# A decoder layer on one core: how the first expert's tokens are picked, where the softmax weights are made, and which row tile comes fourth

## The chip, the core and the metric

The kernel runs on one core of a Trainium2 chip. A core has TensorE (the matrix engine; the profile writes PE for its matmuls and PEld for its weight loads), VectorE (DVE), ScalarE (ACT), GpSimd (POOL), and a queue engine SP that only issues DMAs here. The engines run their own instruction streams and meet at semaphores. The metric is device time in microseconds; lower is better.

## What is computed

One layer of a decoder with 512 prompt rows and 64 sample rows of 1024 numbers, all in float32. Mixing (attention and spatial gating) comes first. The part that matters here starts with its output projection and ends in the expert layer:

```python
    mix = jnp.concatenate([a.reshape(B, S, ATT_W), s_out], axis=-1) @ w_out
    x = x + ga1 * rms_norm(mix, g_post_mix)
    h2 = rms_norm(x, g_pre_ffn) * (1 + sc2) + sh2
    f = hier_moe(h2.reshape(B * S, D_MODEL), ...)
...
def hier_moe(x, w_rg, b_rg, w_re, b_re, w_gate, w_up, w_down):
    g_logits = (x @ w_rg).astype(F32) + b_rg.astype(F32)
    g_prob = jax.nn.softmax(g_logits, axis=-1)
    g_idx = jnp.argmax(g_logits, axis=-1)
    g_w = jnp.take_along_axis(g_prob, g_idx[:, None], axis=-1)
    e_logits = ((x @ w_re).astype(F32) + b_re.astype(F32)).reshape(N, N_EXPERT_GROUPS, EXPERTS_PER_GROUP)
    e_in = jnp.take_along_axis(e_logits, g_idx[:, None, None], axis=1)[:, 0]
    top_p, top_i = lax.top_k(jax.nn.softmax(e_in, axis=-1), TOP_K_IN_GROUP)
    wts = top_p / jnp.sum(top_p, axis=-1, keepdims=True) * g_w
...
    for e in range(N_EXPERTS):
        hdn = jax.nn.silu(x @ w_gate[e]) * (x @ w_up[e])
        y = y + gates[:, e:e + 1] * (hdn @ w_down[e])
```

Each row picks one of four groups, then two of the four experts in it; there are 16 experts, each with 6 MB of weights (`w_gate` and `w_up` 1024 x 512, `w_down` 512 x 1024).

## The kernel before, in words

The program is written out by hand, engine by engine: each engine's function issues its instructions in the order in which they run, and each wait is a semaphore count. No planner sets an order. The stages are `condition`, `project`, `attend_prompt`, `attend_sample`, then `merge` and `experts` in one block, then `later_tiles` and `combine`. The change touches `merge` and `experts`.

**Merge, projection.** The 576 rows are five row tiles: 0 to 3 are the prompt's, 128 rows each, and 4 is the samples', 64 rows. For each tile TensorE transposes the mixed rows (`mix_tr`, L1573), ScalarE and VectorE copy half each out of PSUM (`evac_mix`), and TensorE multiplies with `w_out` (L1611, 32 records of 512 columns). For the samples' tile the two halves of the contraction run side by side on 64 columns each of the array (L1617), and VectorE adds them afterwards (L1425, L1426). Then ScalarE squares and sums (L1359), GpSimd makes the root (`power`, L737, L738), VectorE scales and adds the residual (L1435, L1436), ScalarE squares again (L1365), GpSimd again, and VectorE makes `h2` (L1441, L1442). `h2` is stored to DRAM, transposed on TensorE (`h2_tr_of`, L1584), copied out (L1331, L1397), and multiplied with the router's 20 columns (`logits_of`, L1594). A loop over t interleaves the tiles: TensorE issues projection t, transposes of `h2` t-1, transposes of the mix t+1, logits t-1. `h2` has two buffers `hv`, so ScalarE waits, before it writes one again, for the transposes and the store of the tile two before.

**Merge, routing.** From the logits of all tiles (one instruction covers them all, 128 partitions by 5 tiles by a few columns) VectorE picks the group and the two experts. `first_max` is four operations. In between it waits for ScalarE's two exponentials (L1371, L1373), makes the softmax weights (L1482 to L1486), and writes `hot`, the table of chosen experts (L1489 to L1491). TensorE turns `hot` into ranks, the number of earlier rows that chose the same expert (L1633, L1635). From ranks and totals VectorE orders the experts by their load, gives each a tile of slots, and writes for each row the tile `C` and the place in it `R` (L1496 to L1544). TensorE multiplies the two into a table: which token stands at each place of each tile (L1641). Cast to integers (L1547) it is what GpSimd gathers rows of `h2` with (L1718, L1721).

**Experts.** Sixteen tiles of slots (the first two for experts 0 and 1 at fixed places, then by load, of 128 and 64 rows in turn) run through a loop with two buffers each: gather, transposes (`tokens`, L1795), evacuation of half each (ScalarE L1738, VectorE L1764), gate product (L1812), up product (L1820), `silu` and product, transposes (L1856), down product (L1833) of the tile before, store. Weights go through six slots of the ring; SP issues a load as soon as the product that used the slot is done. The order after the first two experts comes from VectorE (L1553). `step` is in TensorE's order gate, up, next tile's transposes, down of the tile before, transposes of its own. `ORDER`, `first_tokens` and `table` don't exist yet.

## Time and profile before

| | us |
|---|---|
| three runs, median | 1033.86 |
| lowest, highest | 1033.08, 1035.77 |
| the profiled execution | 1031.1 |
| its span | 1029.3 |

| engine | busy, us | share of the span |
|---|---|---|
| TensorE matmuls | 825.5 | 80% |
| TensorE weight loads | 429.3 | 42% |
| VectorE | 345.0 | 34% |
| ScalarE | 210.0 | 20% |
| GpSimd | 121.7 | 12% |

The merge's projection starts at 562 us of the span, the routing at 655, the first expert's gate product at 688.8, and the last down product ends near 988.6. The rest is the combination. A matmul in f32 shows as two records, each with a weight load of its own; a transpose shows as one. In the timeline rows below the columns are start, duration, engine, line, operation, output<-input with the partitions and elements, and the count of merged records; the bracket gives the idle time before it and what ended it. TensorE's clock has two levels, 1.2 and 2.4 GHz; the windows give the granted share, where 0.50 is the lower one.

### The profile page before, as it was taken

The numbers are of one execution on the slowest core, as the hardware profiler recorded it, in microseconds if no ns is written. First come the engines' busy times: TensorE is split into PE (matmuls) and PEld (weight loads), VectorE is DVE, ScalarE is ACT, GpSimd is POOL, SyncE is SP. The second block draws the span as 40 slices with busy tenths as digits, with TensorE's granted clock in tenths as the row PEclk, the third lists the DMA queues.
The fourth block names the chain that finished last, engine by engine and source line by source line (L and its number), as shares of the span: only waits on it lengthen the run. The fifth ranks groups of instructions, "written<-read, shape, count | busy, mean of one in ns | idle before, by whom it ended". The sixth has DMA issues, their size and how long they took to land. (4 is left out here: it accounts for less than half of the span.)

```text
span 1029.3 us, 12324 instructions
## 1 busy us (share of the span) xinstructions
PE 825.5 (80%) x4656; PEld 429.3 (42%) x4656; DVE 345.0 (34%) x799; ACT 210.0 (20%) x437; POOL 121.7 (12%) x204
## 2 busy tenths in 40 slices
PE   0329999999788869899875999249998999999940
PEld 0024444444455545665642455234443444444410
DVE  0143630021578755555530354530110111001017
ACT  0200100100556423433420121100110111111113
POOL 1310100000400011322210010010000000000024
PEclk9959999999679889999986999559999999999975
DMA  8959412382892017999972951514789899999835
GB/s 258 253 165 348 169 56 77 118 305 65 316 401 65 1 61 309 389 414 425 378 285 113 337 223 61 205 62 173 273 327 411 354 388 399 377 415 379 346 115 192
DMA packets 49293, 257.52 MB, mean 250 GB/s; under 512 B 5704, under 2 KB 6952, under 8 KB 38880
## 3 DMA queue, kind: packets, MB, share of 16 engines
q1 hardware_dynamic: 30224, 151.54, 38.7%
q0 software_dynamic: 10672, 86.72, 22.1%
q10 hardware_dynamic: 8352, 18.66, 5.7%
q8 instruction: 29, 0.48, 0.2%
q14 instruction: 16, 0.13, 0.0%
HBM read 234.07 MB, written 22.83 MB: 250 GB/s over the span
## 5 line engine op out<-in xcount | busy, mean ns | idle before, releaser
L695 PE MATMUL ps<-sb 128*128 128x512 f32 x320 | 142.8, 601 | 0.0
L1820 PE MATMUL ps<-sb 128*128 128x512 f32 (+1 forms) x256 | 114.2, 599 | 0.0
L695 PEld LDWEIGHTS ps<-sb 128*128 128x128 f32 x320 | 60.3, 192 | 73.7 <-issue 73.3
L1122 PE MATMUL ps<-sb 128*128 128x128 f32 x512 | 64.9, 281 | 18.4 <-ACT sb L991 9.3
L1774 DVE TENSOR_TENSOR sb<-sb,ps 128x512 f32<-128x512 f32 (+1 forms) x16 | 10.9, 684 | 190.9 <-PE ps L1820 127.6
L1122 PEld LDWEIGHTS ps<-sb 128*128 128x128 f32 x512 | 56.7, 143 | 31.7 <-issue 17.4
L1812 PE MATMUL ps<-sb 128*128 128x512 f32 x144 | 66.8, 618 | 1.0 <-ACT sb L1738 0.8
L1833 PE MATMUL ps<-sb 128*128 128x512 f32 x144 | 63.5, 594 | 0.0
L1611 PE MATMUL ps<-sb 128*128 128x512 f32 x128 | 58.8, 619 | 1.9 <-DVE sb L1389 0.9
L1817 PE MATMUL ps<-sb 128*64 128x512 f32 x112 | 50.9, 608 | 7.5 <-DMA sb<-in_w_up 7.5
L1820 PEld LDWEIGHTS ps<-sb 128*128 128x128 f32 (+1 forms) x256 | 42.5, 168 | 34.4 <-issue 34.4
L879 PE MATMUL ps<-sb 128*128 128x128 f32 (+3 forms) x128 | 53.2, 556 | 3.2 <-ACT sb L792 3.2
L442 PE MATMUL ps<-sb 128*9 128x512 f32 x192 | 22.6, 624 | 39.6 <-DMA sb<-in_w_ada 39.6
L1038 DVE COPY sb<-ps 128x512 f32<-128x512 f32 x64 | 41.2, 685 | 21.0 <-PE ps L1122 21.0
L805 ACT ACTIVATE sb<-sb 128x128 f32<-128x128 f32 (+3 forms) x64 | 35.4, 554 | 41.9 <-DVE sb L859 41.9
L1812 PEld LDWEIGHTS ps<-sb 128*128 128x128 f32 x144 | 27.7, 198 | 33.7 <-issue 31.8
L991 ACT ACTIVATE sb<-ps 128x512 f32<-128x512 f32 x64 | 34.8, 595 | 32.3 <-PE ps L1122 32.0
L1833 PEld LDWEIGHTS ps<-sb 128*128 128x128 f32 x144 | 26.7, 190 | 31.0 <-issue 30.9
L1611 PEld LDWEIGHTS ps<-sb 128*128 128x128 f32 x128 | 25.1, 199 | 32.9 <-issue 30.4
L1781 DVE COPY sb<-ps 128x512 f32<-128x512 f32 (+1 forms) x16 | 11.1, 692 | 77.6 <-PE ps L1833 54.5
L1172 PE MATMUL ps<-sb 128*32 128x256 f32 x512 | 32.2, 404 | 5.8 <-DMA sb<-in_cache_v,ints 4.7
L1135 PE MATMUL ps<-sb 128*32 128x512 f32 (+1 forms) x320 | 36.6, 530 | 0.0
(254 smaller groups left out, 984.2 us busy)
## 6 DMA issues: line engine op xcount, KB each, us to landing
sb<-in_w_gate SPq DMA_DIRECT2D x16, 2048.0 KB, 12.5
sb<-in_w_up SPq DMA_DIRECT2D x16, 2048.0 KB, 16.9
sb<-in_w_down SPq DMA_DIRECT2D x16, 2048.0 KB, 8.4
sb<-in_w_ada SPq DMA_DIRECT2D x12, 2048.0 KB, 12.8
sb<-in_w_in SPq DMA_DIRECT2D x5, 2048.0 KB, 16.6
y_rows<-sb POOLq DMA_DIRECT2D x1, 5120.0 KB, 36.8
y_rows<-sb SPq DMA_DIRECT2D x9, 512.0 KB, 8.8
sb<-in_x_prompt ACTq DMA_DIRECT2D x8, 512.0 KB, 11.9
```

The lines of the kernel that those rows point to most:

```text
L695: last = pe.matmul(PS[:, n % 4, :], L.hT[:, k, t * P:t * P + P], w[:, k, :], start=k == 0, stop=k == KC - 1)
L805: act.activation(pb[n % 3][j][:, 0:w], pb[n % 3][j][:, 0:w], ACT.Exp, bias=nm[:, q:q + 1], accum_out=sums[:, q:q + 1]).then_inc(exp_done, 1)
L879: pe.matmul(PS[:, 2 * (n % 2) + j, 0:P * (i + 1)], qz[i % 2][:, h // 2, 2 * (h % 2) + j, :], L.kT[:, h // 2, 0:P * (i + 1)], start=True, s ...
L991: act.activation(kt[ch % 2][:, h, :], PS[:, h, :], ACT.Copy).then_inc(kt_act, 1)
L1038: dve.tensor_copy(kt[ch % 2][:, h, :], PS[:, h, :]).then_inc(kt_dve, 1)
L1122: last = pe.transpose(PS[:, h, P * g:P * g + P], kp[:, 4 * (ch % 2) + g, P * h:P * h + P], L.cst("ident"))
L1135: last = pe.matmul(bank[32 * h:32 * h + 32, 0:512 if ch < 4 else NS], qst[par][:, h, :], rhs, start=True, stop=True)
L1611: last = pe.matmul(PS[:, proj_bank(t, c), :], mixT[t % 2][:, k, :], w[:, k, :], start=k == 0, stop=k == KC - 1)
L1812: last = pe.matmul(PS[:, 0, :], x[:, k, :], w_gate[:, k, :], start=k == 0, stop=k == KC - 1)
L1817: last = pe.matmul(PS[n:P, 0, :], x[:, k, :], w_gate[:, k, :], start=k == 0, stop=k == KC - 1)
L1820: last = pe.matmul(PS[0:n, 1, :], x[:, k, :], w_up[:, k, :], start=k == 0, stop=k == KC - 1)
L1833: last = pe.matmul(PS[:, 5 + c, :], hT[:, k, :], w[:, k, 512 * c:512 * c + 512], start=k == 0, stop=k == FC - 1)
```

## The change

It does four things. The samples' tile comes fourth and row tile 3 last (`ORDER`); the loops count positions i, and t is the tile at that position. `h2` gets five buffers, on the mixed rows, which are not needed once transposed; the scratch of the routing and the late loads `ga` move elsewhere for it. The softmax weights are made behind the selection instead of inside it, while TensorE makes the ranks. And the tokens of expert 0, whose place is fixed, are no longer gathered with the table: VectorE makes from their ranks a matrix with a one where row and place meet (`first_row`), and TensorE multiplies `h2` with it (`first_tokens`, 40 matmuls), which gives the tokens transposed. The table product moves behind the first gate product, and the gathers start with tile 1. The diff, cut to its core:

```diff
 COLS = (0, 64)
+ORDER = (0, 1, 2, 4, 3)
...
-        hv = [L.at(L.V + D * i, D) for i in range(2)]
+        hv = [L.mix[:, t, :] for t in range(NT)]
...
-        def take(name, n, base=[r0, L.HT + 4096]):
+        def take(name, n, base=[r0, L.V + 2048]):
...
+        self.first_row = L.at(L.HT, NT * P).rearrange("p (t c) -> p t c", t=NT)
+        self.first_done = self.sem("e_first")
...
-        self.ga = [L.at(L.MIX + 2 * D + D * i, D) for i in range(3)]
+        self.ga = [L.at(L.QKT + 512 + D * i, D) for i in range(3)]
         halves, summed = self.sem("e_halves"), self.sem("e_summed")
-        half = L.mix[0:NS, 3, 0:512]
+        half = L.at(L.V, 512, 0, NS)
...
-            sp.wait_ge(halves, 2)
+            sp.wait_ge(proj_done, 4)
...
+            for i, t in enumerate(ORDER):
                 n = rows(t)
                 if t < 4:
-                    act.wait_ge(proj_done, t + 1)
+                    act.wait_ge(proj_done, sum(u < 4 for u in ORDER[:i + 1]))
                 else:
                     act.wait_ge(summed, 2)
-                if t >= 2:
-                    act.wait_ge(h2_tr, t - 1)
-                    act.wait_ge(h2_out2[t % 2], 16 * (t // 2))
-                act.activation(hv[t % 2][0:n], proj(t, n), ACT.Square, accum_out=ss1[0:n, t:t + 1]).then_inc(sq1, 1)
-                if t >= 1:
-                    evac_h2(t - 1)
-                if t + 1 < NT:
-                    evac_mix(t + 1)
-                act.wait_ge(x1_done, t + 1)
-                act.activation(hv[t % 2][0:n], self.x1[0:n, t, :], ACT.Square,
+                act.activation(hv[t][0:n], proj(i, n), ACT.Square, accum_out=ss1[0:n, t:t + 1]).then_inc(sq1, 1)
+                if i >= 1:
+                    evac_h2(i - 1)
+                if i + 1 < NT:
+                    evac_mix(i + 1)
+                act.wait_ge(x1_done, i + 1)
+                act.activation(hv[t][0:n], self.x1[0:n, t, :], ACT.Square,
                                accum_out=ss2[0:n, t:t + 1]).then_inc(sq2, 1)
...
-            act.activation(ee, ee, ACT.Exp).then_inc(exp_out, 1)
-
-            act.wait_ge(tr_done, NT)
+            act.activation(m12, m12, ACT.Exp).then_inc(exp_out, 1)
+
+            act.wait_ge(mod_in, 16 * 5)
+            act.wait_ge(mod_in_s, 16 * 3)
             act.dma_start(self.ga[0], self.mod[NS, 5 * D:6 * D].partition_broadcast(P)).then_inc(self.ga_in, 16)
...
+            for i, t in enumerate(ORDER):
                 n = rows(t)
-                i = 0 if t < 4 else 3
...
-                h = hv[t % 2][0:n]
+                h = hv[t][0:n]
                 if t == 4:
-                    for c in range(2):
-                        bank = proj_bank(t, c)
-                        dve.wait_ge(halves, c + 1)
+                    for f, c in enumerate((i % 2, 1 - i % 2)):
+                        bank = proj_bank(i, c)
+                        dve.wait_ge(halves, f + 1)
                         link(dve.tensor_copy(half, PS[NS:P, bank, :]))
                         dve.tensor_tensor(PS[0:NS, bank, :], PS[0:NS, bank, :], half, ALU.add).then_inc(summed, 1)
-                        dve.wait_ge(summed, c + 1)
...
+                        dve.wait_ge(summed, f + 1)
+                if i >= 1:
+                    evac_h2(i - 1)
+                if i + 1 < NT:
+                    evac_mix(i + 1)
...
+                if i == 3:
+                    link(dve.memset(both[:, 80:96], 0.0))
...
-            dve.tensor_tensor(eg, lg, bc(gm, 4), ALU.subtract).then_inc(exp_in, 1)
             first_max(og, lg, gm)
+            link(dve.memset(og[NS:P, 4, :], 0.0))
...
             link(dve.tensor_tensor(by_group(prod), by_group(le), ogb, ALU.mult))
             link(dve.tensor_reduce(ee, prod.rearrange("p t (g j) -> p t j g", g=4), AX, ALU.add))
-            link(dve.tensor_reduce(gs, ee, AX, ALU.max))
-            dve.tensor_tensor(ee, ee, bc(gs, 4), ALU.subtract).then_inc(exp_in, 1)
-            dve.wait_ge(exp_out, 2)
             link(dve.tensor_reduce(m12[:, :, 0], ee, AX, ALU.max))
             first_max(o1, ee, m12[:, :, 0])
-            link(dve.scalar_tensor_tensor(ee, o1, -2.0, ee, ALU.mult, ALU.add))
+            link(dve.scalar_tensor_tensor(ee, o1, -BIG, ee, ALU.mult, ALU.add))
             link(dve.tensor_reduce(m12[:, :, 1], ee, AX, ALU.max))
             first_max(o2, ee, m12[:, :, 1])
-
+            for j, oj in ((0, o1), (1, o2)):
+                link(dve.tensor_tensor(by_group(hot[:, j]), ogb, oj.unsqueeze(2).to_broadcast([P, NT, 4, 4]), ALU.mult))
+            dve.tensor_tensor(hot[:, 2], hot[:, 0], hot[:, 1], ALU.add).then_inc(hot_done, 1)
+
+            dve.tensor_tensor(eg, lg, bc(gm, 4), ALU.subtract).then_inc(exp_in, 1)
+            link(dve.tensor_tensor(m12[:, :, 1], m12[:, :, 1], m12[:, :, 0], ALU.subtract))
+            dve.memset(m12[:, :, 0], 0.0).then_inc(exp_in, 1)
+            dve.wait_ge(exp_out, 2)
+            link(dve.tensor_reduce(gs, eg, AX, ALU.add))
             link(dve.tensor_tensor(ws, m12[:, :, 0], m12[:, :, 1], ALU.add))
-            link(dve.tensor_reduce(gs, eg, AX, ALU.add))
             link(dve.tensor_tensor(ws, ws, gs, ALU.mult))
             link(dve.reciprocal(ws, ws))
-            link(dve.tensor_tensor(self.weights, m12, bc(ws, 2), ALU.mult))
-            link(dve.memset(both[:, 80:96], 0.0))
-            for j, oj in ((0, o1), (1, o2)):
-                link(dve.tensor_tensor(by_group(hot[:, j]), ogb, oj.unsqueeze(2).to_broadcast([P, NT, 4, 4]), ALU.mult))
-                link(dve.memset(hot[NS:P, j, 4, :], 0.0))
-            dve.tensor_tensor(hot[:, 2], hot[:, 0], hot[:, 1], ALU.add).then_inc(hot_done, 1)
+            dve.tensor_tensor(self.weights, m12, bc(ws, 2), ALU.mult).then_inc(dchain, 1)
+            link.count[0] += 1
 
             dve.wait_ge(rank_done, 1)
+            rank = PS[:, 7, RK:RK + 80].rearrange("p (t e) -> p t e", t=NT)
+            link(dve.scalar_tensor_tensor(rk.unsqueeze(2), rank[:, :, 0:1], 1.0, hot[:, 2, :, 0:1], ALU.add, ALU.mult))
+            dve.scalar_tensor_tensor(self.first_row, L.cst("row").unsqueeze(1).to_broadcast([P, NT, P]), 1.0,
+                                     rk.unsqueeze(2).to_broadcast([P, NT, P]), ALU.add, ALU.is_equal
+                                     ).then_inc(self.first_done, 1)
...
             dve.memset(C[NS:P, 8:10, :], 0.0).then_inc(picks_done, 1)
+            self.expert_evac_x(dve, 0, 0, P)
             dve.tensor_copy(self.ints[:, 32:42], sl)
-            dve.wait_ge(table_made, 1)
+            dve.wait_ge(self.table_made, 1)
...
+                if i >= 1:
+                    logits_of(i - 1)
             h2_tr_of(NT - 1)
             logits_of(NT - 1)
 
@@ -1635,13 +1649,6 @@
                 last = pe.matmul(PS[:, 7, RK + 16 * d:RK + 96], L.cst("ones"), both[:, 0:96 - 16 * d], start=False,
                                  stop=d == NT)
             last.then_inc(rank_done, 1)
-            pe.wait_ge(picks_done, 2)
-            for c in COLS:
-                for n in range(2 * NT):
-                    last = pe.matmul(PS[c:c + 64, 6, 0:NTILE], R[:, n, c:c + 64], C[:, n, :], start=n == 0,
-                                     stop=n == 2 * NT - 1)
-            last.then_inc(table_made, 1)
...
-                pool.wait_ge(ix_done, e + 1)
+                pool.wait_ge(ix_done, e)
...
-            gather(0, 0, P)
-
...
             def tokens(e, par, n):
 
-                pe.wait_ge(xg_in[par], 16 + 8 * (e - par))
-                if differs(e, 0):
-                    pe.wait_ge(xt_a, e)
-                    pe.wait_ge(xt_d, e)
+                pe.wait_ge(xg_in[par], 8 * (e + par))
+                pe.wait_ge(xt_a, e)
+                pe.wait_ge(xt_d, e)
                 if n < P:
                     self.stand_apart(pe)
                 for k in range(KC):
                     last = pe.transpose(PS[:, 2 + k // 4, (k % 4) * n:(k % 4 + 1) * n], B["xg"][par][0:n, k::KC],
                                         L.cst("ident", n)[:, 0:n])
                 last.then_inc(x_tr, 1)
+
+            def first_tokens():
+
+
+                pe.wait_ge(self.first_done, 1)
+                for k in range(KC):
+                    for i, t in enumerate(ORDER):
+                        n = rows(t)
+                        last = pe.matmul(PS[:, 2 + k // 4, (k % 4) * P:(k % 4 + 1) * P], L.mix[0:n, t, k::KC],
+                                         self.first_row[0:n, t, :], start=i == 0, stop=i == NT - 1)
+                last.then_inc(x_tr, 1)
+
+            def table():
+
+
+                pe.wait_ge(self.picks_done, 2)
+                for c in COLS:
+                    for n in range(2 * NT):
+                        last = pe.matmul(PS[c:c + 64, 6, 0:NTILE], self.R[:, n, c:c + 64], self.C[:, n, :],
+                                         start=n == 0, stop=n == 2 * NT - 1)
+                last.then_inc(self.table_made, 1)
...
                     last.then_inc(g_done, 1)
+                if not differs(e, 0):
+                    table()
                 w_up = weights(EXPERT[par][1], e, par, KC)
...
-            tokens(0, 0, P)
+            first_tokens()
             looped(pe, step)
```

TensorE at the end of the projection, before: projection of row tile 3 (128x512), then the samples' (64x512), and what follows up to the ranks.

```order
L1611 MATMUL ps<-sb 128x512 x16
L1584 MATMUL ps<-sb 128x128 x8
L1573 MATMUL ps<-sb 128x64 x8
L1594 MATMUL ps<-sb 64x20 x16
L1617 MATMUL ps<-sb 64x512 x16
L1584 MATMUL ps<-sb 128x128 x8
L1594 MATMUL ps<-sb 64x20 x16
L1584 MATMUL ps<-sb 128x64 x8
L1594 MATMUL ps<-sb 64x20 x8
```

With the change, the same place:

```order
L1631 MATMUL ps<-sb 64x512 x16
L1597 MATMUL ps<-sb 128x128 x8
L1585 MATMUL ps<-sb 128x128 x8
L1608 MATMUL ps<-sb 64x20 x16
L1625 MATMUL ps<-sb 128x512 x16
L1597 MATMUL ps<-sb 128x64 x8
L1608 MATMUL ps<-sb 64x20 x8
L1597 MATMUL ps<-sb 128x128 x8
L1608 MATMUL ps<-sb 64x20 x16
```

The samples' product (64x512) moved in front of the last full one, and the last transposes and logits are those of a tile of 128 rows: 128x128 and 64x20 x16 instead of 128x64 and 64x20 x8.

TensorE from the last rank product (L1635, L1649) to the transposes of the second expert's tokens, before:

```order
L1635 MATMUL ps<-sb 128x16
L1641 MATMUL ps<-sb 64x26 x20
L1784 UNCONDITIONAL_BRANCH
L1795 MATMUL ps<-sb 128x128 x8
L1812 MATMUL ps<-sb 128x512 x8
L1820 MATMUL ps<-sb 128x512 x8
L1795 MATMUL ps<-sb 128x128 x8
```

With the change:

```order
L1649 MATMUL ps<-sb 128x16
L1791 UNCONDITIONAL_BRANCH
L1812 MATMUL ps<-sb 128x128 x40
L1839 MATMUL ps<-sb 128x512 x8
L1822 MATMUL ps<-sb 64x26 x20
L1849 MATMUL ps<-sb 128x512 x8
L1801 MATMUL ps<-sb 128x128 x8
```

The table product (64x26 x20) moved from ahead of the expert stage to between gate and up; 40 products of 128x128 stand where 8 transposes stood.

VectorE between the selection of experts and the first operation on the totals (L1496, L1507), before:

```order
L1482 TENSOR_TENSOR sb<-sb 128x5
L1483 TENSOR_REDUCE sb<-sb 128x5
L1484 TENSOR_TENSOR sb<-sb 128x5
L1485 RECIPROCAL sb<-sb 128x5
L1486 TENSOR_TENSOR sb<-sb 128x10
L1487 MEMSET sb 128x16
L1489 TENSOR_TENSOR sb<-sb 128x80
L1490 MEMSET sb 64x16
L1489 TENSOR_TENSOR sb<-sb 128x80
L1490 MEMSET sb 64x16
L1491 TENSOR_TENSOR sb<-sb 128x80
L1496 SCALAR_TENSOR_TENSOR sb<-ps,sb 128x16
```

With the change:

```order
L1486 TENSOR_TENSOR sb<-sb 128x80
L1488 TENSOR_TENSOR sb<-sb 128x20
L1489 TENSOR_TENSOR sb<-sb 128x5
L1490 MEMSET sb 128x5
L1492 TENSOR_REDUCE sb<-sb 128x5
L1493 TENSOR_TENSOR sb<-sb 128x5
L1494 TENSOR_TENSOR sb<-sb 128x5
L1495 RECIPROCAL sb<-sb 128x5
L1496 TENSOR_TENSOR sb<-sb 128x10
L1501 SCALAR_TENSOR_TENSOR sb<-ps,sb 128x5
L1502 SCALAR_TENSOR_TENSOR sb<-sb 128x640
L1507 SCALAR_TENSOR_TENSOR sb<-ps,sb 128x16
```

The table `hot` (128x80) is written ahead of the weights (128x5, 128x10) instead of behind them, and two operations on ranks, the second of 640 elements, now stand before the first on the totals.

## Rows read from the trace of the kernel before

**Rows 1.** Windows: stretch, us, busy PE PEld DVE ACT POOL, clock, DMA share, GB/s

```profile
646.00:686.00 40.00, 9.83 (x77) 9.33 (x77) 22.39 (x85) 1.97 (x5) 3.34 (x6) 0.51 0.35 123
...
706.00:786.00 80.00, 79.88 (x245) 36.64 (x244) 8.05 (x14) 8.72 (x17) 5.67 (x10) 1.00 0.76 298
```

**Rows 2.** Waits from 686 to 1029 us: who <- released by, total us, times, longest

```profile
PE ps L1817 <- DMA sb<-in_w_up: 7.5, 4, 4.0
```

**Rows 3.** Timeline, end of the projection: start, duration, engine, line

```profile
616.03 14.00 PE L1611 MATMUL ps<-sb 128*128 128x512 f32 x32
...
633.54 7.06 PE L1617 MATMUL ps<-sb 128*64 128x512 f32 x31
...
641.72 0.69 DVE L1426 TENSOR_TENSOR ps<-ps,sb 64x512 f32<-64x512 f32 x1
642.45 1.02 ACT L1359 ACTIVATE sb<-ps 64x1024 f32<-64x1024 f32 x1 [6.42 <-DVE ps L1426]
```

**Rows 4.** Timeline, logits of tile 3, then transposes and logits of the samples' tile

```profile
644.09 1.83 PE L1594 MATMUL ps<-sb 128*64 128x20 f32 x32 [2.40 <-ACT sb L1331]
...
651.71 1.14 PE L1584 MATMUL ps<-sb 64*128 64x64 f32 x8 [5.79 <-DVE sb L1442]
...
653.46 1.87 PE L1594 MATMUL ps<-sb 128*64 128x20 f32 x16 [0.61 <-DVE sb L1397]
```

**Rows 5.** Timeline, routing up to the rank product

```profile
657.31 0.17 DVE L1473 TENSOR_REDUCE sb<-sb 128x5 f32<-128x20 f32 x1
...
658.19 0.18 DVE L1459 TENSOR_TENSOR sb<-sb 128x20 f32<-128x20 f32 x1
...
660.31 0.17 DVE L1482 TENSOR_TENSOR sb<-sb 128x5 f32<-128x5 f32 x1
...
661.38 0.07 DVE L1487 MEMSET sb<- 128x16 f32 x1
...
662.61 0.74 PE L1633 MATMUL ps<-sb 128*128 128x96 f32 x2 [7.28 <-DVE sb L1491]
...
663.15 2.21 PE L1635 MATMUL ps<-sb 128*128 128x80 f32 x10
```

**Rows 6.** Timeline, from the ranks to the second tile's gate product

```profile
665.39 0.17 DVE L1496 SCALAR_TENSOR_TENSOR sb<-ps,sb 128x16 f32<-128x16 f32 x1 [2.84 <-PE ps L1635]
...
674.08 1.49 DVE L1537 TENSOR_TENSOR sb<-sb 128x1280 f32<-128x1280 f32 x1
...
676.14 4.07 PE L1641 MATMUL ps<-sb 128*64 128x26 f32 x40 [10.78 <-DVE sb L1544]
...
686.00 1.97 PE L1795 MATMUL ps<-sb 128*128 128x128 f32 x8 [5.79 <-DMA sb<-h_rows,ints]
...
688.00 0.69 DVE L1764 COPY sb<-ps 128x512 f32<-128x512 f32 x1 [4.69 <-PE ps L1795]
...
688.80 9.86 PE L1812 MATMUL ps<-sb 128*128 128x512 f32 x16 [0.83 <-ACT sb L1738]
...
698.86 0.36 SPq L1211 DMA_DIRECT2D sb<-in_w_gate  x1
...
705.36 1.05 PE L1795 MATMUL ps<-sb 128*128 128x128 f32 x8
...
707.25 7.10 PE L1812 MATMUL ps<-sb 128*128 128x512 f32 x16
```

**Rows 7.** Prompt attention's first weight loads; where the clock rises: timeline and windows

```profile
266.89 2.63 PEld L879 LDWEIGHTS ps<-sb 128*128 128x128 f32 x12 [3.30 <-issue]
...
266.90:268.00 1.10, 1.08 (x5) 0.50 0.99 417
...
694.00:695.00 1.00, 1.00 (x3) 0.53 (x2) 0.00 (x0) 0.00 (x0) 0.00 (x0) 0.82 0.00 0
...
790.55 1.11 PE L1817 MATMUL ps<-sb 128*64 128x512 f32 x1 [4.00 <-DMA sb<-in_w_up]
...
793.00:794.00 1.00, 1.00 (x6) 0.37 (x4) 0.00 (x0) 0.00 (x0) 0.00 (x0) 0.83 0.91 377
```

187 lines of the change are left out of this document (93 added, 94 removed).

## The prediction

> **What bounds the kernel now.** I read the table of stretches first [rows 1]. From 706 to 786 us, with the experts running, TensorE is busy 79.9 of 80 us. From 646 to 686 us it is busy 9.8 of 40 us, at a granted clock of 0.51: here one chain runs through VectorE, ScalarE, GpSimd and a DMA, and TensorE waits. Next the waits from 686 us on [rows 2]: TensorE waits for weights only 7.5 us in all (4 times, at most 4.0), and once, 5.8 us, for the gather of the first tile [rows 6]. So behind the first tile the end is set by TensorE's own work, and what the chain in front loses or gains arrives at the end, provided the weight loads move along. They do: each is released by a product of the same loop.
>
> The changed region has three pieces: the end of the projection [rows 3, 4], the routing up to the rank product [rows 5], and the way from the ranks to the first expert [rows 6]. I sum along that chain, in the time of the profiled execution.
>
> **1. The samples' tile fourth, row tile 3 last.** Before, the projection of row tile 3 starts at 616.03 and the samples' at 633.54, ending 640.60 [rows 3]. Their two halves must then be added on VectorE; the last add ends 642.41, and ScalarE's square starts at 642.45, 1.85 us after the product. With a full tile last the square follows the product by some 0.2 us: a gain of 1.65. But the halves now stand in the middle. Samples' product ends about 616.03 + 7.2 = 623.2; the second copy and add (0.69 each) run until 624.98; ScalarE squares from there, and evacuates tile 2's h2 after it, which is 1.02 [rows 3] and about 0.6 more, at 626.6. TensorE meanwhile makes two sets of transposes, until about 625.2, and then stands still for 1.4 us before the logits and the last product. That product ends near 642.2, the square starts near 642.4, as before: the 1.65 are spent on the standstill and on transposes of the mix that are now of a full tile. Everything to the transposes of the last h2 (651.71 in [rows 4]) has the same durations, since a row operation costs the same for 64 and 128 partitions. **Term: 0.0.**
>
> After 651.71 the last tile is twice as tall. The clock is at half level (0.51 over the stretch, [rows 1]). The eight transposes of 64 columns took 1.14 us [rows 4]; eight full ones at the half clock took 1.97 [rows 6], so +0.8. The evacuation is of 512 columns (0.69 in [rows 6]) instead of 256: +0.3 as my estimate. The logits are 32 records instead of 16; 16 took 1.87 us, between 0.11 and 0.12 each: +1.8. **Term: +2.9.** The other end is 0.2: 32 records took 1.83 us at the full clock [rows 4], if it should be granted. I take 2.9, because TensorE stands idle here about as long as before.
>
> **2. Softmax off the chain.** Between 657.31 and 658.19 VectorE takes a maximum, subtracts, waits for ScalarE's exponential and takes the next maximum. Only the last of these is still needed before the selection, 0.2 of the 0.88: 0.67 goes. The weights' five operations, 660.31 to 661.38, go: 1.07 [rows 5]. So do the maximum's subtraction for the first exponential (0.1), and the memsets, net 0.3. **Term: -2.1.** They now stand behind the selection, while TensorE makes the rank product, which lasts from 662.61 to 665.36 [rows 5], 2.75 us. Needed there: two subtractions and a memset 0.5, two exponentials with their handovers some 0.5, five operations 1.05; 2.1 of 2.75. If that cover were short, each missing us would be one lost. ScalarE's three DMA issues wait for nobody.
>
> **3. Ranks to the first expert's tokens.** Before: VectorE from 665.39 until the table product starts at 676.14, that product 4.07, a cast, a copy on GpSimd, the gather, transposes at 686.00, evacuation, and the first gate product at 688.80 [rows 6]: 23.4 us after the ranks. Now: one small operation (0.2) and one over 640 elements. The nearest row has 1280 elements in 1.49 us; half is 0.75. With the handover 1.05.
>
> Then the new product: 8 x 5 matmuls, each two records as elsewhere in f32, so 80 records with weights of 128 columns and 128 moving columns. Its price is the main unknown. The nearest row is one of twelve weight loads of that shape, each with such a product, in 2.63 us at a clock of 0.50: 0.22 each [rows 7]. At the full clock a record of 512 columns halves, 7.10 us for 16 against 9.86 for 16 mostly at half [rows 6], so I take 0.11. The clock starts at half. In the expert's start it rose 5.6 us after the dense work began at 688.80 (0.82 in the us 694 to 695); after the 4.0 us stall it rose 2.6 us after 790.55 (0.83 in 793 to 794) [rows 7]. I take 5.6: 25 records in it, 55 x 0.11 = 6.05 behind it, **11.65 us in all**. Ends: 2.6 us of half clock gives 10.1; all at half clock 17.6.
>
> VectorE, working on the slots meanwhile, is 0.95 late and free 11.7 us after the ranks; the product ends at 1.05 + 11.65 = 12.7, so it waits for the product and not the reverse. With the evacuation (0.69, [rows 6]) and two handovers 13.65 to the gate product. **Term: 13.65 - 23.4 = -9.8.** If the clock came early, VectorE's 11.7 would bound it: at most one us more gain.
>
> **4. From gate to the next tokens.** Before 705.36 - 688.80 = 16.56 us, with the gate product partly at half clock. Now gate 6.9 and up 6.9 at full clock, and the table product between them: 40 records at 0.057 (1.83 / 32, [rows 4]), 2.25. **Term: -0.5.** The gather of tile 1 hangs on this table. It took 5.8 us from the table to the transposes before (680.2 to 686.0, [rows 6]); the up product covers 6.9. If that cover is gone, it costs what the gather is late. SP waits for the order of the experts, which VectorE makes behind the table; expert 2's first load, at 698.86 before [rows 6], is then issued some 7 us earlier, although it no longer follows the gate product at once. Its data is used by the third tile only, behind all of the second one, which began at 707.25, so this is hidden.
>
> Waits on the stores and transposes of h2 disappear with the five buffers; ScalarE started its squares right behind the products before, so nothing is gained. Moving scratch and the three late loads costs nothing: the queues idle there.
>
> **Sum:** 0.0 + 2.9 - 2.1 - 9.8 - 0.5 = **-9.5 us**. On the profiled execution 1031.1 becomes 1021.6; it lay 2.8 below the median of the three runs (1033.86), so the median should be 1024.4, -0.9%.
>
> **Rivals.** A: the same mechanism with the half clock held through the whole product: 17.6 instead of 11.65, and the sum is -3.6, 1030.3. For it: the clock stayed at half from 646 to 694, past bursts of 4 us. Against: from the ranks on this is continuous work. B: weight loads don't overlap the products. Each record then costs load plus stream, 0.44 at half and 0.22 at full clock: 13 in the first 5.6 us and 67 x 0.22 = 14.7, together 20.3; the sum is -0.8, 1033.0. Against it, strongly: 0.22 per record in [rows 7] at half clock already contains both. The Trainium skill, "TensorE: Matmul & The Clock Gate", section "The mechanism", states such a rule: weight loads overlap running matmuls only where their row groups differ, and here all use the same rows. By that rule this rival holds; the trace disagrees. C, the slower side: the short products, which accumulate five tiles into one place, wait for each other, load and then stream, and with gaps between them the clock never rises: 0.44 throughout, 35.2 us, and the sum is +14.1, 1047.9. It turns from gain to loss above 21 us, 0.26 a record. For it: the clock stayed at half through the 4.07 us of the table's short products [rows 6]. Against: the expert's products accumulate eight deep and run back to back. D: the last tile meets the full clock, or the clock rises early: -10.5 for the second, -12.2 for the first, -13.2 for both: 1020.7 to 1023.4. E: a late gather or longer waits for weights (the 4.0 us stall falls differently) moves the sum by 2 either way.
>
> **Chances.** Forecast with E 0.70, D 0.12, A 0.10, B 0.04, C 0.04. A measurement of this kernel can tell about 0.3% from no change, 3.1 us. Forecast and D are beyond that, and half of A: faster 0.87; half of A and most of B within: same 0.09; C: slower 0.04. The range 1020.0 to 1029.0 holds D's larger part, the forecast with E's two us and the spread of the runs; it leaves out most of A, B and C.
>
> **What would show it.** Right: the last h2 transposes near 652, logits of 32 records lasting 3.5 us; the rank product starting about 0.8 us later than 662.6; 80 records from some 667.5, in about 12 us, with the clock rising inside; the gate product near 679.5; TensorE without a gap between up and the next transposes; the loop's later waits near 7.5 us. Wrong: a product over 20 us, the clock still at half in the gate product, a wait on the gather of tile 1, or longer waits for weights.

## The result, and the profile after

The changed kernel takes 1039.04 us in the median of 20 runs (1033.08 to 1048.66), the kernel before, run beside it, 1033.37 (20 runs): a ratio of 1.0051, 95% interval 1.0033 to 1.0069. One of the 20 runs, the 1048.66, was a slow execution and is left out of the ratio. The changed kernel is half a per cent slower, where 0.9% faster was forecast. The profiled execution took 1038.27 us, its span is 1036.5, against 1031.1 and 1029.3.

The timeline of the changed kernel, from the end of the projection to the second tile (columns as in the rows of before). It is 0.69 us late at 612.99, ahead of everything that the change moves.

```profile
612.99 1.04 PE L1597 MATMUL ps<-sb 128*128 128x128 f32 x8
...
627.23 1.83 PE L1608 MATMUL ps<-sb 128*64 128x20 f32 x32 [1.54 <-ACT sb L1336]
...
652.37 1.97 PE L1597 MATMUL ps<-sb 128*128 128x128 f32 x8 [6.60 <-DVE sb L1446]
655.21 3.17 PE L1608 MATMUL ps<-sb 128*64 128x20 f32 x32 [0.87 <-DVE sb L1400]
...
658.42 0.18 DVE L1407 TENSOR_TENSOR sb<-ps,sb 128x20 f32<-128x20 f32 x1 [3.36 <-PE ps L1608]
...
663.59 0.74 PE L1647 MATMUL ps<-sb 128*128 128x96 f32 x2 [5.21 <-DVE sb L1486]
...
664.94 0.17 DVE L1496 TENSOR_TENSOR sb<-sb 128x10 f32<-128x10 f32 x1
666.37 0.16 DVE L1501 SCALAR_TENSOR_TENSOR sb<-ps,sb 128x5 f32<-128x5 f32 x1 [1.26 <-PE ps L1649]
666.57 0.82 DVE L1502 SCALAR_TENSOR_TENSOR sb<-sb 128x640 f32<-128x640 f32 x1
...
692.46 10.10 PE L1839 MATMUL ps<-sb 128*128 128x512 f32 x16 [0.83 <-ACT sb L1751]
702.49 2.31 PE L1822 MATMUL ps<-sb 128*64 128x26 f32 x40
704.72 7.13 PE L1849 MATMUL ps<-sb 128*128 128x512 f32 x16
711.69 1.04 PE L1801 MATMUL ps<-sb 128*128 128x128 f32 x8
```

Between 666.57 and 692.46 stand the 40 new matmuls of `first_tokens` (L1812). From here on they are called the product, or the rank product; the sum that makes the ranks themselves (L1647, L1649) is called the ranks or the rank sum. The group of the product's weight loads, from the one-line view (duration ns least, median, most; first and last start), the timeline of these loads at its beginning, and windows over it (stretch, us, busy PE, clock, DMA share, GB/s). A window counts a record that crosses its edge on both sides, so the counts in brackets are one or two too high:

```profile
L1812 PEld LDWEIGHTS ps<-sb x80: 309/335/338, 667.4 to 691.0; 128*128 128x128 f32 x64, 64*128 64x128 f32 x16
```

```profile
667.45 1.52 PEld L1812 LDWEIGHTS ps<-sb 128*128 128x128 f32 x6 [1.22 <-DVE sb L1502]
669.18 0.55 PEld L1812 LDWEIGHTS ps<-sb 64*128 64x128 f32 x2 [0.22 <-issue]
669.95 2.00 PEld L1812 LDWEIGHTS ps<-sb 128*128 128x128 f32 x8 [0.22 <-issue]
672.17 0.55 PEld L1812 LDWEIGHTS ps<-sb 64*128 64x128 f32 x2 [0.22 <-issue]
```

```profile
670.00:690.00 20.00, 20.00 (x69) 0.50 0.02 6
690.00:695.00 5.00, 4.17 (x8) 0.50 0.00 0
695.00:700.00 5.00, 5.00 (x9) 0.65 0.00 0
```

The reader is to see three things: the 80 records take from 667.45 until 24.2 us later, 0.30 us each; the loads pause 0.22 us at every step from a 128-row tile to the 64-row tile and back, 16 times; and the clock is at 0.50 through all of it and into the gate product behind.

By stage, against [rows 4], [rows 5] and [rows 6]:

| stage | before | after | difference | forecast |
|---|---|---|---|---|
| to the last h2 transposes, less the 0.69 | 651.71 | 651.68 | 0.0 | 0.0 |
| these transposes until VectorE reads the logits | 3.66 | 6.05 | +2.4 | +2.9 |
| from there to the rank sum's first record | 7.24 | 5.17 | -2.1 | -2.1 |
| ranks to the gate product | 23.41 | 26.09 | +2.7 | -9.8 |
| gate product to the next tokens | 16.56 | 19.23 | +2.7 | -0.5 |

(Before's logits are read at 655.37. The rank sum itself, 2.78 us until VectorE reads it, is the same in both.) The sum is +5.7. With 0.69 in front and 0.2 more waiting for the up weights (7.7 us, against 7.5 in [rows 2]) that is 6.6 of the 7.2 us between the spans. The miss of 15 us is in two rows, 12.5 in the product and 3.2 behind it.

### The profile page after: what moved, and what is told of

It reads as the page before. It is cut to its first block and busy times, and to the rows that moved or that the text cites. A ratio compares the mean times of both kernels' runs of the same rounds, so it can differ in the third digit from the quotient of the medians.

```text
span 1036.5 us, 12458 instructions
## 1 busy us (share of the span) xinstructions
PE 847.6 (82%) x4728; PEld 446.0 (43%) x4728; DVE 344.6 (33%) x800; ACT 210.0 (20%) x437; POOL 120.6 (12%) x202
## 5 line engine op out<-in xcount | busy, mean ns | idle before, releaser
L880 PE MATMUL ps<-sb 128*128 128x128 f32 (+3 forms) x128 | 50.7, 534 | 3.2 <-ACT sb L793 3.2
## 6 DMA issues: line engine op xcount, KB each, us to landing
sb<-in_w_in SPq DMA_DIRECT2D x5, 2048.0 KB, 16.4
```

Source lines behind the costliest of these rows:

```text
L880: pe.matmul(PS[:, 2 * (n % 2) + j, 0:P * (i + 1)], qz[i % 2][:, h // 2, 2 * (h % 2) + j, :], L.kT[:, h // 2, 0:P * (i + 1)], start=True, s ...
```

## The experiments

Theory at first: the changes of height of the products (the 64-row tile) stop TensorE and hold the clock down (call it H). Rivals: the clock at entry (K), the roles of the two operands, the moved order. All kernels are the changed kernel with the edit shown, unless another is named, and the edits are cut to their core; each is compared with the kernel before, run beside it. The groups of experiments ran at different times, so their medians in us are not to be compared with one another, only the ratios. Below each expectation stands what was measured.

**e1: all tiles at full height.** The 64 missing rows of the samples' tile are filled with zeros.

```diff
+                    link(dve.memset(L.mix[NS:P, 4, :], 0.0))
...
-                        ... L.mix[0:n, t, k::KC],
-                                         self.first_row[0:n, t, :], ...
+                        ... L.mix[:, t, k::KC],
+                                         self.first_row[:, t, :], ...
```

> The changed kernel, but the samples' tile enters the new product as a full tile: its 64 missing rows are set to zero once on VectorE, and all 80 records of the product have 128 rows. Theory H (in the trace of the changed kernel the weight loads stand still about 0.33 us at each change between 128 and 64 rows, 16 changes, 5.3 us): the product falls from 24.2 to about 19 us, and the time from 1039 to about 1034. Rival R (the price of 0.30 a record comes from accumulating in one place, or from reading every eighth column): the product stays at 24 us and the time at 1039. In both the clock stays at half level in it.

Measured: 1031.98 us, ratio 1.000 (0.9975 to 1.0025). Timeline of TensorE, then windows over the product, split where the clock rises (stretch, us, busy PE, busy PEld, clock, DMA share, GB/s):

```profile
665.97 19.36 PE L1813 MATMUL ps<-sb 128*128 128x128 f32 x80 [1.11 <-DVE sb L1503]
686.16 7.11 PE L1840 MATMUL ps<-sb 128*128 128x512 f32 x16 [0.83 <-ACT sb L1752]
```

```profile
665.97:670.93 4.96, 4.96 (x20) 4.96 (x21) 0.50 0.54 160
670.93:685.33 14.40, 14.40 (x61) 14.21 (x60) 1.00 0.00 0
```

The product is 4.8 us shorter, as H had it. The clock, which was expected to stay at half, rises 4.96 us into it, and the gate product is back at 7.11. So the changes of height cost 4.8 us there and 3.0 behind. But 19.36 is far from 11.65, and the windows say why the clock isn't the answer: some 20 records in 4.96 us at half clock, some 60 in 14.40 at full clock. A record costs 0.24 us at either level.

**e2: the full clock at entry.** Idle products of 512 columns fill TensorE's waits: 7 ahead of the last transposes, 5 behind the logits.

```diff
+            def heat(n):
+                for _ in range(n):
+                    pe.matmul(PS[:, 0, :], L.cst("ident"), L.cst("dist"), start=True, stop=True)
...
+            heat(7)
             h2_tr_of(NT - 1)
             logits_of(NT - 1)
+            heat(5)
```

> The changed kernel with idle TensorE time filled: 7 products of 512 columns (14 records) into a bank that nobody reads, before the last h2 transposes, and 5 before the rank product. Nothing of the result depends on them. Theory K (the half clock at the entry is what doubled the product, the last logits, the ranks and the gate product): clock 1.00 from 640 to the expert stage, product about 12 to 15 us instead of 24.2, logits 1.8 instead of 3.2, ranks 1.5 instead of 2.8, gate 7.1 instead of 10.1; in all some 15 us, near 1024. Rival K2 (short products let the clock fall whatever it was before): it falls inside the product, which takes 18 us or more, and the gate product is still slow: 1031 to 1034. Rival K3 (the filling products delay the chain): logits or ranks start later than 652.4 and 663.6 by more than 1 us.

Measured: 1033.75 us, ratio 1.0016 (0.9987 to 1.0044). Timeline, then windows:

```profile
654.43 1.81 PE L1608 MATMUL ps<-sb 128*64 128x20 f32 x32 [0.88 <-DVE sb L1400]
...
664.06 24.19 PE L1818 MATMUL ps<-sb 128*128 128x128 f32 x80 [1.11 <-DVE sb L1502]
```

```profile
664.06:664.69 0.63, 0.63 (x3) 1.00 0.99 260
664.69:688.25 23.56, 23.56 (x79) 0.50 0.14 33
```

The logits nearly halve (1.81 for 3.17), but the product takes 24.19 again, and the kernel 1033.75 where K had some 1024. The clock is at full level when the product starts, falls 0.63 us later and is not back before the gate product. So the clock at entry is not what makes the product long, and K is out. The fall comes after some three records, before the first 64-row tile (665.80): the changes of height can't have brought it about, and no run here shows what did.

**e3: roles swapped.** The one-hot matrix is the weights, the rows of h2 move, 512 columns at a time; then an evacuation and eight transposes.

```diff
-                for k in range(KC):
+                for c in range(2):
                     for i, t in enumerate(ORDER):
                         n = rows(t)
-                        last = pe.matmul(PS[:, 2 + k // 4, (k % 4) * P:(k % 4 + 1) * P], L.mix[0:n, t, k::KC],
-                                         self.first_row[0:n, t, :], start=i == 0, stop=i == NT - 1)
+                        last = pe.matmul(PS[:, 2 + c, :], self.first_row[0:n, t, :],
+                                         L.mix[0:n, t, 512 * c:512 * c + 512], start=i == 0, stop=i == NT - 1)
...
```

> The changed kernel, but the new product takes the one-hot matrix as weights and the rows of h2 as moving data: 20 records of 512 columns give the tokens as rows, which are copied out and transposed by 8 transposes, as a gathered tile is. Theory C (the clock rises under 512-column products as it did in the gate product, 5.6 us after they begin, and did not rise in 24 us of 128-column products): product about 11 to 12 us, with copy, transposes and copy about 15 us from the ranks to the gate product instead of 26.1, gate 7.1 instead of 10.1: near 1025. Rival T (the clock goes by time since TensorE was last idle for long, not by the kind of product): product 17 us, about 21 to the gate product, gate 7.1 to 10: 1031 to 1034.

Measured: 1024.09 us, ratio 0.9922 (0.9887 to 0.9957). Timeline, from the product to the gate product:

```profile
664.68 11.72 PE L1817 MATMUL ps<-sb 128*128 128x512 f32 x20 [1.11 <-DVE sb L1503]
677.28 1.13 PE L1823 MATMUL ps<-sb 128*128 128x128 f32 x8 [0.88 <-DVE sb L1557]
679.24 7.11 PE L1850 MATMUL ps<-sb 128*128 128x512 f32 x16 [0.83 <-ACT sb L1754]
```

So the rank product can win some 8 us against the kernel before; its form lost them. The 64-row tile is still in it, with 4 changes of height, and the clock rises at 668.9, 4.2 us into it, all the same.

**e4: the samples' tile last again**, `ORDER = (0, 1, 2, 3, 4)`, and the up load waiting for both halves.

> The changed kernel with the order of the row tiles undone (samples' tile last again); SP's wait before the slots of w_out is that of the kernel before. By the traces of before and after the order cost 2.4 us at the last transposes and logits and gained nothing ahead of them: 1036.6. Inside the new product the samples are now last, with as many changes of height as before: 24 us. Rival (the order gains what its place suggests, the two halves' addition leaves the chain): 1040 to 1041.

Measured: 1032.98 us, ratio 1.003 (0.9997 to 1.0064). From the last transposes (647.78) to the rank sum (656.59) 8.81 us, where the changed kernel has 11.22: the taller last tile costs 2.4 us, as the table above says. The product takes 23.95, so the order has no part in the miss. The 1036.6 that I expected was reckoned from the changed kernel's 1039.04, which is of another group of runs. Against the kernel before, e4 is 0.3% slower and the changed kernel 0.5%: that fits 2.4 us, but the two intervals overlap, so it rests on the traces.

**f1 and f2: what sets 0.24 us a record.** Both on e1's kernel.

```diff
-L.mix[:, t, k::KC]                               # e1
+L.mix[:, t, k * P:(k + 1) * P]                   # f1: adjacent columns
-self.first_row[:, t, :]                          # e1
+self.first_row[:, t, 0:64]                       # f2: half of the moving columns
```

These two, and g1, g3 and h1 below, only ask for a price and are no versions: with other columns as weights the first expert gets its columns in a wrong sequence, and f2 leaves half of that expert's tokens out. Sizes and waits are as in e1.

> This kernel is the one with the samples' tile filled up to 128 rows with zeros, and in it the rank product takes as weights 128 columns that lie side by side (k*128 to k*128+127) in place of every eighth one. The expert then gets its columns in another sequence, so that part of the computation is changed; sizes, waits and numbers of instructions are the same. What is disputed is the price of a product with 128 moving columns, 0.24 us a record in the padded kernel at 1.2 and at 2.4 GHz alike, while its weight loads stand back to back. Theory S (the stride of the weights is what costs: 32 bytes from one element to the next): the product falls from 19.36 us to under 13, with records at 0.11 to 0.15 us once the clock is up. Theory L (loading 128x128 weights of a true f32 product costs that much, whatever their stride): 19.4 us again, 0.24 a record.

> This kernel is the padded one, and in it the rank product streams only the first 64 of the 128 one-hot columns against each loaded tile of weights; the other 64 tokens of the first expert's tile are then whatever the bank held, so half of that product is left out. Theory L (the weight load sets the pace): 80 records stay at 0.24 us, the product at 19.4 us. Rival B (load and stream follow each other, neither beside the other): a record loses the 64 columns' stream, 0.05 us at 2.4 GHz and 0.11 at 1.2 by half of the 0.22 us that a 128-column record took at half clock in the kernel before: about 15 us. Theory of the stream alone: 0.12 us a record, 9.7 us.

Measured, f1: 1024.86 us, ratio 0.994 (0.9903 to 0.9977). f2: 1034.15, 1.0026 (1.0000 to 1.0052). First f1's products and windows (columns as for e1, split where the clock rises), then f2's product:

```profile
668.59 11.18 PE L1813 MATMUL ps<-sb 128*128 128x128 f32 x80 [1.11 <-DVE sb L1503]
680.60 7.11 PE L1840 MATMUL ps<-sb 128*128 128x512 f32 x16 [0.83 <-ACT sb L1752]
```

```profile
668.59:672.79 4.20, 4.20 (x19) 4.20 (x20) 0.50 0.68 176
672.79:679.77 6.98, 6.98 (x63) 6.79 (x61) 1.00 0.00 0
```

```profile
665.05 19.37 PE L1813 MATMUL ps<-sb 128*128 128x64 f32 x80 [1.11 <-DVE sb L1503]
```

With every tile at full height, this is the cause of the larger part. With adjacent columns the product takes 11.18 us, 0.213 a record at half clock and 0.112 once the clock is up (some 61 in 6.98; the starts of the records in the trace give the third digit); with every eighth column it takes 19.36. In f2 half the stream changes nothing, so it is the weight load that sets the pace. In f2, though, the clock stays at 0.50 through the product, and its gate product takes 9.68, so this test holds for half clock. For full clock f1 shows it: there the same 128 moving columns pass in 0.11 us, so the 0.24 of e1 isn't their time.

**g1: adjacent columns, the 64-row tile as it is.** f1's edit of the columns, on the changed kernel itself.

> This kernel is the changed one, with its 64-row tile, and only the weights of the rank product are other columns of the same rows: 128 that lie side by side in place of every eighth one (the first expert then gets its columns in another sequence, so that part of the computation is changed). In the padded kernel the same edit took the product from 19.36 to 11.18 us. If the 16 changes of height cost 0.30 us each on top whatever the weights' stride (4.82 us by the changed kernel against the padded one), the product takes 11.2 + 4.8 = 16.0 us and the gate comes at 24.18 - 16.0 = 8.2 us earlier after the ranks. If the standstill belongs to the stride (the next strided load cannot be taken up ahead at a change of height, and an adjacent one is short), it is 11.2 + 16 x 0.11 = 13 us at most. If the stops keep the clock down, the gate takes 9 to 10 us in place of 7.1.

Measured: 1029.66 us, ratio 0.9952 (0.993 to 0.9974). Timeline of TensorE:

```profile
668.73 17.57 PE L1812 MATMUL ps<-sb 128*128 128x128 f32 x80 [1.11 <-DVE sb L1502]
687.13 7.11 PE L1839 MATMUL ps<-sb 128*128 128x512 f32 x16 [0.83 <-ACT sb L1751]
```

Its weight loads, to be held against those of the changed kernel above, and its windows (columns as for e1, split where the clock rises):

```profile
671.03 1.78 PEld L1812 LDWEIGHTS ps<-sb 128*128 128x128 f32 x8 [0.23 <-issue]
673.03 0.50 PEld L1812 LDWEIGHTS ps<-sb 64*128 64x128 f32 x2 [0.22 <-issue]
```

```profile
668.73:680.48 11.75, 11.75 (x44) 9.95 (x45) 0.50 0.22 59
680.48:686.30 5.82, 5.82 (x38) 4.67 (x37) 1.00 0.00 0
```

I expected 16.0 or 13; it is 17.57, 6.4 above f1. The pauses stay whatever the stride, and with them the clock stays at half for 11.75 us, where it did for 4.20 in f1. The windows also give the price of a pause at both levels, 8 changes of height in each: 44 records at f1's 0.213 are 9.4 of the 11.75 us, which leaves about 0.3 a change at half clock; 37 records at f1's 0.112 are 4.1 of the 5.82 us, which leaves about 0.2 at full clock. At half clock the stride costs almost nothing (2.00 us for eight loads in the changed kernel, 1.78 here): it shows only where the clock is up.

**f3 and g2: half as many changes of height.** The five tiles are taken in opposite sequence for every second k.

```diff
-for i, t in enumerate(ORDER):
+for i, t in enumerate(ORDER[::1 - 2 * (k % 2)]):                             # f3
+for i, t in enumerate((0, 1, 2, 3, 4) if k % 2 else (4, 3, 2, 1, 0)):        # g2
```

> This kernel is the changed one, and in it the five tiles are taken in the opposite sequence for every second k, so that the 64-row tile of one k stands beside that of the next and the height of the products changes 8 times in place of 16. The sums are the same. If a change of height costs 0.33 us of standstill (the changed kernel's 24.18 us against 19.36 with all tiles at full height, 4.82 us over 16 changes, 0.30 each), the product takes 24.2 - 2.4 = 21.8 us and the kernel comes 2 to 3 us earlier. If what costs is the number of 64-row products or the clock they hold down, and not the change, it stays at 24.2 us. If the fewer stops let the clock rise, gate and table come out at 7.1 and 2.3 us as well and 3 us more are gained.

> This kernel is the changed one with the tiles of the rank product taken as 4, 3, 2, 1, 0 for even k and 0 to 4 for odd k, so that the 64-row tile of one k now does stand beside that of the next, and the height of the products changes 8 times in place of 16 (the run f3 kept the two changes for each k, since the 64-row tile stands fourth and not last in the sequence that it turned round). If a change of height costs 0.30 us, the product takes 24.2 - 2.4 = 21.8 us. If what costs is each 64-row product itself and not the change, it stays at 24.2 us.

f3 doesn't do what it was meant to: the 64-row tile stands fourth in `ORDER`, so turning it round leaves 16 changes. It measured 1037.08 us (1.0056, 1.0033 to 1.008) with 23.89 us for the product, and says only that the sequence as such does little. g2: 1037.48 us (1.0027, 1.0008 to 1.0045). Its timeline:

```profile
669.27 21.51 PE L1812 MATMUL ps<-sb 64*128 64x128 f32 x80 [1.12 <-DVE sb L1502]
691.61 8.62 PE L1839 MATMUL ps<-sb 128*128 128x512 f32 x16 [0.83 <-ACT sb L1751]
```

24.18 - 21.51 = 2.67 us for the 8 changes that went, 0.33 each, and 21.51 - 19.36 = 2.15 for the 8 that stayed, 0.27 each. The clock went up and down in it (0.50 to 674.2, then 1.00, 0.50 from 677.6 and 1.00 from 684.4 to 687.8), which may account for part of the difference. In g2 the later waits for the up weights came to 11.2 us instead of 7.7, which hides the gain in the whole: the profiled execution, at 1041.41, was the slowest of its ten.

**g3 and h1: two other distances**, on e1's kernel: every second column (8 bytes apart), every fourth (16 bytes).

```diff
-L.mix[:, t, k::KC]
+L.mix[:, t, k // 2 * 256 + k % 2:(k // 2 + 1) * 256:2]        # g3
+L.mix[:, t, k // 4 * 512 + k % 4:(k // 4 + 1) * 512:4]        # h1
```

> This kernel is the padded one with every second column as weights (8 bytes from one element to the next) in place of every eighth one (32 bytes); the first expert gets its columns in another sequence. With 32 bytes the product took 19.36 us at 0.24 us a record, with 4 bytes 11.18 us. If any stride costs alike, it is 19.4 us again. If the price grows with the distance, it lies between: about 12 to 14 us if it grows evenly with the bytes. If it costs only from some distance on, it is 11.2 us.

> This kernel is the padded one with every fourth column as weights (16 bytes from one element to the next); the first expert gets its columns in another sequence. Adjacent columns took 11.18 us, 8 bytes 11.88, 32 bytes 19.36. The Trainium skill, page SBUF - State Buffer, section Door 1: The DMA port swizzle, says that accesses within one line of 16 bytes have full bandwidth, that two hits in a line are needed for it, and also that four float32 elements can be strided over for free. By the two hits a distance of 16 bytes pays in full, since no two elements share a line: 19.4 us. By the last half sentence it is free: 11.2 to 11.9 us. If the price grows evenly with the distance, without any line: 8 bytes cost 0.7 us, so 16 bytes cost 2 to 4 us: 13 to 15 us.

Measured, g3: 1021.89 us (two runs only), ratio 0.9877 (0.9837 to 0.9918); h1: 1031.17, 0.9974 (0.995 to 0.9999). g3's product, then h1's:

```profile
666.41 11.88 PE L1813 MATMUL ps<-sb 128*128 128x128 f32 x80 [1.11 <-DVE sb L1503]
```

```profile
667.27 18.93 PE L1813 MATMUL ps<-sb 128*128 128x128 f32 x80 [1.12 <-DVE sb L1503]
```

Distances of 4, 8, 16 and 32 bytes give 11.18, 11.88, 18.93 and 19.36 us: not even growth, but a step between 8 and 16. Of the 0.70 us between the first two about half is the clock, which rose 4.2 us into f1's product and 4.9 us into g3's; at full clock a record is 0.112 in f1 and 0.118 in g3. The Trainium skill, "SBUF — State Buffer", section "Door 1: The DMA port swizzle", has the rule: lines of 16 bytes, and at least two hits in each for the full rate. These four runs agree with that. They disagree with the half sentence behind it, that a distance of 4 float32 is free.

**h2: full height and the full clock at entry**: e1's and e2's edits together.

> This kernel is the padded one (every eighth column as weights, all tiles at full height) with 7 idle products of 512 columns ahead of the last transposes and 5 behind the logits, so that the rank product starts at the full clock. If a strided record costs 0.24 us whatever the clock (the theory), the product takes 19.4 us again, and the clock stays at 1.00 through it, since without changes of height TensorE has no stops. If the first part of the 19.36 us was long because of the half clock, it takes 17 us or less. If the clock falls in it as it fell in e2, it is the strided loads and not the changes of height that bring it down. The kernel as a whole: logits and ranks 2.8 us shorter than in the padded kernel, 1029 us.

Measured: 1030.04 us, ratio 0.9946 (0.9914 to 0.9977). Timeline of TensorE and windows (columns as for e1, split where the clock changes):

```profile
670.51 19.34 PE L1819 MATMUL ps<-sb 128*128 128x128 f32 x80 [1.11 <-DVE sb L1503]
```

```profile
670.51:673.31 2.80, 2.80 (x12) 2.80 (x12) 1.00 0.51 155
673.31:676.72 3.41, 3.41 (x16) 3.41 (x16) 0.50 0.00 0
676.72:689.85 13.13, 13.13 (x56) 12.94 (x55) 1.00 0.00 0
```

19.34 again, with 15.9 of it at full clock: the strided record costs 0.24 us at both levels. I expected the clock to stay at 1.00, and it didn't: it falls here too, without any change of height, but is back after 3.4 us, where in e2 it stayed at 0.50 for the other 23.56 us of the product. The two kernels differ in nothing but the height of one tile, so that is what I put the staying down to; it is one execution of each, and in h2 the clock had already been at 0.50 from 659.7 to 666.5, ahead of the product. There the second lot of idle products took 7.38 us for 10 records (4.56 in e2) and held up the ranks, so little of the 2.8 us that were expected from logits and ranks arrived in this execution.

**f4, g4 and h3: versions.** f4 is e3 with the samples last. g4 keeps the product's form but lets ScalarE first make copies with regrouped columns, so that the weights are adjacent, and has the samples last, at full height. h3 is g4 with the last copy behind the exponents and with 5, 5 and 1 idle products.

```diff
+for t in range(NT):
+    act.activation(self.side[t].rearrange("p (k c) -> p k c", k=KC),
+                   L.mix[:, t, :].rearrange("p (c k) -> p k c", k=KC), ACT.Copy).then_inc(self.side_done, 1)
...
-L.mix[0:n, t, k::KC]
+self.side[t][:, k * P:(k + 1) * P]
```

> This kernel has the roles in the rank product swapped (one-hot as weights, normalised rows as the moving 512 columns, then eight transposes) and the samples' tile back in the last place. If the two effects add up: the swap alone gave 1024.09 us against 1031.81 before (ratio 0.992); from the last transposes to the ranks the samples-last order took 8.81 us where the changed order took 11.22, which is 2.4 us less; that gives 1021.7 us, ratio 0.990. Against it: in the samples-last order the later waits for the up weights were 9.3 us where they were 7.7 in the changed order, and the product began 1.6 us before the clock had a chance to rise; if those eat the 2.4 us, it comes out at 1024, ratio 0.992, the same as with the swap alone.

> This kernel has the samples' tile back in the last place and filled up to 128 rows with zeros, and ScalarE, idle between the last evacuation and the exponents, makes a copy of each tile of normalised rows with the columns regrouped (five copies of 128x1024, about 1.05 us each by the 1.05 of other 128x1024 copies), so that the rank product reads 128 adjacent columns as weights and writes the expert's columns in the right sequence, with neither strides nor changes of height nor transposes. If the copies are hidden (5.3 us beside VectorE's 9 us of routing), ranks to gate takes 11.2 + 2.8 = 14 us, against 16.8 with swapped roles and 26.1 in the changed kernel, and the time is 2.5 us under that of the swapped kernel with the samples last: 1021.56 - 2.5 = 1019 us, ratio about 0.989. If ScalarE's read of every eighth column is slow (over 1.6 us a copy), the exponents and the ranks are late by what the copies run past, and it is no faster than 1021.6.

> This kernel is g4 with two edits. ScalarE makes the copy of the samples' tile behind its exponents and not ahead of them, since its five copies of every eighth column took 1.97 us each, in place of the 1.05 that I had reckoned, and held VectorE up for 2.5 us; and 5, 5 and 1 idle products of 512 columns fill TensorE's idle time ahead of the last transposes, behind the logits and behind the ranks. The first edit should bring the rank product 1.7 us earlier. The second: logits 1.87 to 0.95, ranks 2.9 to 1.7, the product from 10.83 to 80 x 0.111 = 8.9 us, 4 us together. Expected 1022.4 - 5.7 = 1016.7 us, ratio 0.983. If the idle products end too late, or the clock falls between the logits and the product, the second gains nothing and it is 1020.7.

| | us | ratio | interval |
|---|---|---|---|
| f4 | 1021.56 | 0.9913 | 0.9885 to 0.9941 |
| g4 | 1022.36 | 0.9879 | 0.9851 to 0.9907 |
| h3 | 1022.87 | 0.9900 | 0.9853 to 0.9946 |

All three beat the kernel before by about 1%, the changed kernel by more, and can't be told apart, nor from e3. f4 came out as expected (1021.7); g4 was expected at 1019 and h3 at 1016.7, and both missed. g4's timeline, then h3's:

```profile
652.87 7.88 ACT L1375 ACTIVATE sb<-sb 128x1024 f32<-128x1024 f32 x4
660.65 2.07 ACT L1375 ACTIVATE sb<-sb 128x1024 f32<-128x1024 f32 x1
...
664.95 10.83 PE L1819 MATMUL ps<-sb 128*128 128x128 f32 x80 [1.99 <-DVE sb L1508]
676.61 7.11 PE L1846 MATMUL ps<-sb 128*128 128x512 f32 x16 [0.83 <-ACT sb L1757]
```

```profile
667.41 9.17 PE L1828 MATMUL ps<-sb 128*128 128x128 f32 x80 [1.16 <-DVE sb L1510]
677.92 0.69 DVE L1682 COPY sb<-ps 128x512 f32<-128x512 f32 x1
678.72 7.11 PE L1855 MATMUL ps<-sb 128*128 128x512 f32 x16 [2.13 <-issue]
```

My reckoning of g4 missed by the same effect that it was to avoid: ScalarE's copies read every eighth column and took 1.97 us each, not 1.05, so VectorE waited 2.50 us for the exponents, until 662.97. TensorE had made the ranks meanwhile, and the product started some 0.9 us late (its wait is 1.99 us, against 1.11 in the other runs). In h3 the product is down to 9.17 us at the full clock, but then VectorE, still making slots until 677.9, evacuates late, and the gate product waits 2.13 us, where 0.83 is usual. Its idle products ahead of the last transposes ran mostly at half clock (10 records in 6.50 us, where e2's 14 took 6.28), and the transposes start only when they end.

## Why the prediction was wrong, step by step

**Term 1, order: right** (0.0, with the standstill of 1.54 us at 627.23 where 1.4 was forecast). The taller last tile cost 2.4 where 2.9 stood: the 32 logits took 3.17 us, not 3.7.

**Term 2, softmax off the chain: right**, -2.1, and its cover held: the weights are done at 665.1, and VectorE reads the ranks at 666.37, after waiting 1.26 us for them.

**Term 3 failed, and there one step: "At the full clock a record of 512 columns halves, ... so I take 0.11".** The row of 0.22 [rows 7] has adjacent weights. At half clock that hides the difference, since a strided record costs 0.24 and an adjacent one 0.21. At full clock it doesn't: adjacent gives 0.11 and 11.18 us for the product (f1), within half a us of the forecast's 11.65, but every eighth column stays at 0.24. I had priced a shape, 128x128, and not how it is read; the diff says `k::KC` in plain sight. This is 8.2 us of the 12.5 missed (19.36 - 11.18). Another 4.8 (24.18 - 19.36) are the 16 pauses at changes of height, 0.30 us each. They stood in no term. The remaining half us of the difference went the other way. The split depends on what is mended first, because each of the two spoils what mending the other gives. With the stride mended first (g1) it is 6.6 us for the stride (24.18 - 17.57) and 6.4 for the pauses (17.57 - 11.18), since the pauses also keep the clock down, which costs adjacent loads and not strided ones. Either alone would have taken half of the gain or more: the ratio is 1.000 with the stride alone (e1) and 0.9952 with the pauses alone (g1), where 0.991 was forecast.

**The clock.** The forecast let it rise 5.6 us into the product. In f1, with neither stride nor pauses, it did after 4.2 us. With stride and 16 pauses it stayed at half for all of the product and beyond, as rival A had it (changed kernel, e2, e4). At full height it rose after 5.0 us even with the stride (e1). So the pauses keep it down, but the rule behind it is not found: with pauses and adjacent columns it rose after 11.75 us (g1), with 8 pauses it went up and down (g2), and with half the moving columns and no pause at all it stayed at half (f2).

**Term 4 is the clock again**: gate product 10.10 instead of 6.9, +3.2. Of this 0.2 is my own: 6.9 was too low for the full clock, for which [rows 6] has 7.10. Where the clock was up (e1), the gate product took 7.11, the table 2.31 and the up product 7.13, 16.4 to the next tokens against the 16.1 that the forecast makes. The gather of tile 1 was covered, as said.

**The rivals.** B and C gave serial loads and streams, 0.22 to 0.44 a record. Neither is the mechanism: in f1, 80 loads that are 10.99 us busy stand within 11.18 us of products, and at full clock a record of 128 columns takes 0.11 us, a quarter of the 0.44 that one of 512 columns takes (7.11 for 16), which leaves no time for a load ahead of it. That also speaks against the rule of the Trainium skill that B cited ("TensorE: Matmul & The Clock Gate", section "The mechanism"): the loads overlap on the same rows, and pause just where the number of rows changes. C's break-even (21 us, 0.26 a record) was right as arithmetic: the product took 24.2 and the change lost. Its chance of 0.04, with B's, was too low for a product whose like had no row at full clock.

## What to carry to other kernels

Price a matmul by how its weights are read, not only by their shape: with float32 elements 16 or 32 bytes apart the load, and not the stream, set the pace of a product with 128 moving columns, and the higher clock gave nothing back (0.24 us a record in e1 and h2 at either level). Swap the operands so that adjacent columns move, or regroup the strided one first on an engine with time to spare (here at twice the price of an adjacent pass). Do not mix tile heights inside a loop of short products; zeros up to the full height were cheaper than the changes (ratio 1.000 in e1, 1.0051 without them). And two faults in one product hide each other: e1 alone or g1 alone would each have shown only part of the loss.
